# One subtraction behind the product of gates in a product-key retrieval, on one core of a Trainium2

## The reference

```python
s1 = jnp.einsum('thd,hnd->thn', q[:, :, 0], k1)      # 128 scores per token, twice
s2 = jnp.einsum('thd,hnd->thn', q[:, :, 1], k2)
t1, i1 = lax.top_k(s1, 16)
t2, i2 = lax.top_k(s2, 16)
cand_s = t1[..., :, None] + t2[..., None, :]         # 16 x 16 candidates
cand_i = i1[..., :, None] * 128 + i2[..., None, :]
top_s, top_pos = lax.top_k(cand_s, 16)
expert = jnp.take_along_axis(cand_i, top_pos, axis=-1)
gate = jax.nn.softmax(top_s, axis=-1)
```

## Time and profile before

| | |
|---|---|
| median of three executions | 3253.53 us |
| lowest and highest | 3252.69 and 3258.23 us |
| the profiled execution | 3256.87 us, its span 3255.2 us |
| granted clock of TensorE, mean | 0.914 |
| VectorE busy, 5075 instructions | 2411.1 us, 74% of the span |
| GpSimd busy, 1196 instructions | 1637.7 us, 50% |
| TensorE busy | 2668.9 us, 82% |
| the retrieval's heads | about 776 to 1120 us from the span's start |

### The profile page before, as it was taken

How to read it: one execution, slowest core, us unless ns; L and a number is a source line. 1 busy time by engine, 2 the same in 40 slices (tenths; PEclk the granted TensorE clock), 3 DMA queues, 4 the chain that set the end, 5 groups by cost and what they waited for, 6 DMA issues and landing times.

```text
span 3255.2 us, 40544 instructions
## 1 busy us (share of the span) xinstructions
PE 2668.9 (82%) x14888; PEld 2079.1 (64%) x14888; DVE 2411.1 (74%) x5075; ACT 952.6 (29%) x1327; POOL 1637.7 (50%) x1196
## 2 busy tenths in 40 slices
PE   7996688868888366663676999999999999998886
PEld 6886567757666255552444777676667766767774
DVE  4511666644999899994677777787877877779999
ACT  4311433322444334442111222222222222222222
POOL 0001011012777655553666674666665777755674
PEclk9988799989888677886788999999999999999998
DMA  4223322122110279887999998999999999998995
GB/s 133 90 85 98 101 82 69 55 78 83 56 50 21 86 255 310 294 292 279 408 390 384 393 384 329 387 389 396 385 387 338 404 409 406 394 391 298 339 341 180
DMA packets 309933, 833.93 MB, mean 256 GB/s; under 512 B 26128, under 2 KB 114640, under 8 KB 309744
## 3 DMA queue, kind: packets, MB, share of 16 engines
q0 software_dynamic: 150864, 548.60, 44.1%
q1 hardware_dynamic: 158880, 282.83, 24.8%
HBM read 772.45 MB, written 58.88 MB: 255 GB/s over the span
## 4 chain that ended last, share of the span: by engine, by line
DVE 14%; DMA 13%; POOL 10%; PE 9%; issue 6%; ACT 0%; POOLq 0%; DVEq 0%; ACTq 0%
DMA e_u_row<-in_u,id_u 13%; POOL hold L1827 7%; DVE e_u_row L2046 4%; POOL e_u_row L1818 3%; DVE e_y L2036 3%; PE psum L1888 2%; PE psum L1889 1%; PE psum L1890 1%; DVE e_ul L2002 1%; PE psum L1867 1%; PE psum L1869 1%; PE psum L1868 1%; DVE e_vl L2006 1%; DVE hold L2055 1%; DVE e_al L2023 1%
## 5 line engine op out<-in xcount | busy, mean ns | idle before, releaser
L2046 DVE CUSTOM_DVE_ANT_0 e_u_row<-e_u_row,hold 128x1024 f32<-128x1024 f32 x384 | 467.6, 1223 | 275.1 <-DMA e_u_row<-in_u,id_u 240.4
L1818 POOL DMA_INDIRECT e_u_row<-in_u,id_u x384 | 484.1, 1261 | 352.9 <-DVE hidden_s L2046 231.9
L1888 PE MATMUL psum<-e_vh,e_ah 128*128 128x512 f32 x1024 | 427.4, 417 | 144.2 <-DVE e_y L2036 109.9
L1827 POOL DMA_INDIRECT hold<-in_v,id_v x384 | 439.4, 1144 | 141.6 <-issue 113.1
L1889 PE MATMUL psum<-e_vl,e_ah 128*128 128x512 f32 x1024 | 414.2, 405 | 0.0
L1890 PE MATMUL psum<-e_vh,e_al 128*128 128x512 f32 x1024 | 412.3, 403 | 0.0
L1888 PEld LDWEIGHTS psum<-e_vh,e_ah 128*128 128x128 f32 x1024 | 201.0, 196 | 256.5 <-DVE e_y L2036 144.8
L1867 PE MATMUL psum<-x1d_hi,e_uh 128*128 128x512 f32 x864 | 341.0, 395 | 0.0
L1868 PE MATMUL psum<-x1d_lo,e_uh 128*128 128x512 f32 x864 | 337.2, 390 | 0.0
L2036 DVE TENSOR_TENSOR e_y<-e_y,psum 128x512 f32<-128x512 f32 x504 | 323.7, 679 | 18.1 <-PE psum L1890 16.8
L1869 PE MATMUL psum<-x1d_hi,e_ul 128*128 128x512 f32 x864 | 336.3, 389 | 0.0
(11 more groups left out here) (332 smaller groups left out, 5625.2 us busy)
## 6 DMA issues: line engine op xcount, KB each, us to landing
e_vr<-in_v SPq DMA_DIRECT2D x128, 512.0 KB
e_ur<-in_uT SPq DMA_DIRECT2D x108, 512.0 KB
s_G<-g_tile SPq DMA_DIRECT2D x8, 4096.0 KB, 26.3
e_g<-s_G SPq DMA_DIRECT2D x64, 512.0 KB
p_wr<-in_w_ch SPq DMA_DIRECT2D x17, 512.0 KB, 3.9
s_ch<-p_out POOLq DMA_DIRECT2D x16, 512.0 KB, 4.1
m_ch<-s_ch SPq DMA_DIRECT2D x8, 1024.0 KB, 5.9
r_w<-in_wq SPq DMA_DIRECT2D x16, 512.0 KB
```

The source lines that it names most:

```text
L1818: pool.indirect_dma_start(out=u_ring[n % U_RING][:], out_offset=None, in_=io["u"], in_offset=bass.IndirectOffsetOnAxis(ap=id_u[:, s, k:k + ...
L1827: pool.indirect_dma_start(out=v_ring[m % V_RING], out_offset=None, in_=io["v"], in_offset=bass.IndirectOffsetOnAxis(ap=id_v[:, t:t + 1], a ...
L1888: nc.tensor.matmul(acc, ah[s][j][:, r], vh[s][j][:, c], start=(j == 0), stop=False)
L2046: nc.vector.tensor_tensor_reduce(row, row, xs[:, s, :], 1.0, 0.0, ALU.mult, ALU.add, hs[:, s, k:k + 1]).then_inc(dotted, 1)
```

## The change

In each `head` of VectorE's program the wait for `p_first` and the subtraction of line 1400, which releases `p_ready[v]`, move behind the reciprocal (1402) and the product of gates (1404). Nothing else is changed.

```diff
                     dve.wait_ge(p_base, h + 1)
                     nc.vector.scalar_tensor_tensor(psh[:], pf[v][0][:], float(TOPK), psh[:], ALU.mult, ALU.min).then_inc(p_first, 1)
-                    dve.wait_ge(p_first, h + 1)
-                    nc.vector.tensor_tensor(pf[v][1][:], pf[v][1][:], psh[:], ALU.subtract).then_inc(p_ready[v], 1)
                     dve.wait_ge(g_sum, h + 1)
                     nc.vector.reciprocal(gsum[:], gsum[:]).then_inc(g_rec, 1)
                     dve.wait_ge(g_rec, h + 1)
                     nc.vector.tensor_tensor(gate[:, :, ts(h * TOPK, TOPK)], ex[:],
                                             gsum[:, :].unsqueeze(2).broadcast_to([P, NT, TOPK]),
                                             ALU.mult).then_inc(g_out, 1)
+                    dve.wait_ge(p_first, h + 1)
+                    nc.vector.tensor_tensor(pf[v][1][:], pf[v][1][:], psh[:], ALU.subtract).then_inc(p_ready[v], 1)
```

## The result

The changed kernel takes 3262.35 us where the kernel before takes 3255.18, medians of 20 executions each. The ratio is 1.0017, with a 95% interval of 1.0009 to 1.0025: 5.5 us slower, between 2.9 and 8.1 (the two medians by themselves lie 7.2 us apart). That is a little more than the 4.2 us forecast. The prediction held that only some 0.2%, 6.5 us, can be told from no change; with 20 executions each the 5.5 us are under that, and still clear of zero.

A forecast was written before the change was run, and what follows sets the result against it. VectorE was taken to set the retrieval's pace, partly locked out by GpSimd. Terms 1.55 - 0.41 + 0.48 + 0.31 + 2.24 = +4.2 us on the 3253.5 median gave 3257.7 us, range 3248 to 3263.

The forecast's parts named there:

- 1.: End of each head: product about 0.29 us instead of 3.77, next maxima 3.6 us earlier, GpSimd's lookup 0.31 us later.
- 2. and 3.: Casts and line 1321: the 3.6 us return as waits for GpSimd; heads 0 to 4 lose 0.31 us each.
- the loop: Positions ready, GpSimd's lookups and first split, line 1321, rest of the head on VectorE, positions ready; only 0.31 us changes.
- 4. and 5.: Head 5 to 6, without a GpSimd split, gains 0.41 us; head 6, product still locked out, costs 0.48 us.
- 6.: Tail: line 1418 likely starts before GpSimd's half and holds it up 2.24 us, plus 0.31 for the later start.
- Rival A: Retrieval: the waits don't grow and seven products give 3.48 us each, -24.4 us, 3229 us; 8%.
- B: Line 1321 slips ahead of GpSimd's split: -7.3 us over five heads, sum -4.7, 3249 us; 8%.
- C: Line 1321 waits for GpSimd's second split too, 2.34 us more in five heads: +11.7 and +4.2, 3269 us; 7%.
- Rival D: Retrieval: the 0.31 us is hidden and the tail goes GpSimd's way, 0 to +2 us; 22%.
- the sum: Whole retrieval: 1.55 - 0.41 + 0.48 + 0.31 + 2.24 = +4.2 us; +1.9 with GpSimd first in the tail.

The follow-up runs named there:

- no_product: Kernel before without VectorE's product of gates, ScalarE copying the undivided exponentials into the gates instead: ratio 0.9996 to the kernel before.
- spare_maxima: Changed kernel plus eight extra maxima ahead of line 1329 in heads 1 to 7: head 0's line 1398 to line 1432's end 309.77 us, not 310.15.
- split_moved_after: Changed kernel with line 1321's split moved behind the index searches of line 1377: 3244.19 us, ratio 0.9962 to the kernel before.
- gpsimd_first_by_more: Changed kernel plus four extra reciprocals ahead of line 1418, GpSimd starting 0.15 us ahead: tail 21.66 us instead of 23.77.
- the last run: Changed kernel with line 1321's split moved, GpSimd's line 1439 splits behind the positions (heads 0 to 5), exponential moved earlier: 3224.65 us, ratio 0.9903.

## Why the prediction was right

The numbers are those of the prediction's places.

1. The product took 0.29 us, the maxima came at 0.85 and the lookups at 1.01 us behind line 1398, all as worked out; in head 6 it stayed locked out (2.45 us).
2. and 3. The 3.6 us come back as waits, and the loop has none of the product in it. Three runs show it: the product can be left out of the kernel before for nothing (no_product), 1.5 us per head can be added to the changed one for nothing (spare_maxima), and the loop shortens when the one wait that closes it goes (split_moved_after). The five heads lost 0.28 to 0.32 us each, 0.31 forecast.
4. and 5. Head 5 to 6 measured -0.39 (forecast -0.41), head 6 to 7 +0.37 (+0.48): in head 6 the lookups start 0.40 us later, not 0.48.
6. The tail measured +2.41 (forecast 2.24 + 0.31); gpsimd_first_by_more, with the same order and another start, took 2.1 of it back. The exclusive port of the Trainium skill (SBUF — State Buffer, section SBUF: two separate sides) is borne out here, with the first to start as its holder: the late one ends 3.5 us (GpSimd, 3.66 undisturbed) or 2.1 us (VectorE, 2.29) after the first is done.

TensorE, forecast as covered, was: between 818 and 1105 us VectorE waits for no other engine, in all 1.7 us and only for itself. Rival A (the gain stays) would have given D = 282: out. B needed 1.21 us at line 1321 and C some 5.3 (2.95 + 2.34); the measured 2.95 us excludes both. Rival D (nothing to be seen) is out as well: the 0.31 us was not hidden, and the tail went VectorE's way. What the sum had no term for is the distance between 4.2 and the measured 5.5 us; the interval holds both, the stage's own +3.91 doesn't ask for more, and no run says whether the rest is real.

Two things were less good than the sum. The absolute time was forecast as 3257.7 and came out at 3262.35, near the upper end of the range: 1.65 us of that is the base, a median of three executions that twenty moved up to 3255.18. And "VectorE sets the pace of the retrieval", read from its busy share and its missing waits, doesn't hold as it stands: in the changed kernel ten microseconds more of work on VectorE cost nothing. The pace is set by the loop through both engines, which the prediction's own steps 2 and 3 then worked out.

The moved subtraction is the one that releases GpSimd's lookups, but the change doesn't release them earlier. It releases VectorE from GpSimd, and GpSimd starts 0.31 us later.

## What to carry to other kernels

An operation that another engine holds up is worth its wait only if nothing further on waits for the same engine: before taking such a stall away, follow the loop from one release to the next, and count only what stands in it. An engine that is busy for 97% of a stretch may be spending a good part of it locked out; the same instruction at two durations is the sign. What such an edit is worth depends on how the two engines lie against each other: the same order of instructions cost 3.9 us of D here, and gained 19.8 once the lookups started later. Where two engines share a port, shift one against the other so that the long operations of the one meet the steps of the other that don't need it: here that, with the split and the exponential moved, took 26 us off D, where moving the split alone took 4.8 (old order) or 7.1 (the change's order).

## What the runs showed of the hardware that was not expected

- A few hundredths of a microsecond decide who waits. Line 1418 starting 0.04 us ahead of GpSimd's operation lengthens that one by 2.1 us; starting 0.15 us behind, it is itself lengthened by 3.4 us (5.65 instead of 2.29). Only the wait on GpSimd's side lengthens the stage. The prediction had called the first likely, but no row of before showed it.
- A small instruction put ahead of a wait can cost nothing at all: with one reciprocal of 0.20 us more, line 1418 started 0.05 us ahead of GpSimd, where it had been 0.04, and D was 310.00 instead of 310.15.
- Starting GpSimd's lookups 4.6 us later made a head 3.7 us shorter (39.6 in split_moved_after to 35.9 in the last run), though nobody does less work. The exponential had to move for it, but the gain isn't the exponential's own: in split_moved_after VectorE never waits for it from head 1 on.
